# Differential attention heads: fp32 products against three f16 products of halves and remainders

## What is computed

```python
def block(args):
    q_blk, i = args                      # 128 queries
    ...
    logits = jnp.einsum('bqhmd,bkhmd->bhmqk', q_blk, k).astype(jnp.float32) * scale + bias
    p = jax.nn.softmax(logits, axis=-1)
    attn = p[:, :, 0] - lam * p[:, :, 1]
    return jnp.einsum('bhqk,bkhd->bqhd', attn.astype(v.dtype), v)
```

## Time and profile before

| what | before |
| --- | --- |
| median of 3 runs | 2670.33 us (2670.31 to 2670.44) |
| span of the profiled execution | 2668.5 us |
| PE busy | 2656.6 us, 100% |
| DVE busy | 1822.5 us, 68% |
| ACT busy | 1337.7 us, 50% |
| POOL busy | 136.5 us, 5% |

### The profile page before, as it was taken

One profiled execution on the slowest core, in us unless ns is written; L12 is line 12 of the kernel. 1 busy time (PEld: TensorE's weight loads), 2 busy tenths in 40 slices (PEclk: granted clock), 3 DMA queues, 4 the chain that ended last, 5 costly groups with the idle time before them and its releaser, 6 DMA issues.

```text
span 2668.5 us, 45121 instructions
## 1 busy us (share of the span) xinstructions
PE 2656.6 (100%) x17772; PEld 1741.6 (65%) x17772; DVE 1822.5 (68%) x2792; ACT 1337.7 (50%) x2284; POOL 136.5 (5%) x119
## 2 busy tenths in 40 slices
PE   9999999999999999999999999999999999999999
PEld 6886476654688646886476654688646556465664
DVE  7995385666899528994385665899526786557854
ACT  5664265552566425663265542566424654336452
POOL 1000012100100001000022100100000002000020
PEclk9999999999999999999999999999999999999999
DMA  5443321223344333443322223444323232321312
GB/s 170 115 121 107 122 80 59 88 67 104 91 120 116 116 98 95 121 115 107 122 80 67 81 74 104 116 125 111 121 100 119 72 95 72 111 84 64 111 64 87
DMA packets 313358, 266.23 MB, mean 100 GB/s; under 512 B 8796, under 2 KB 276316, under 8 KB 312576
## 3 DMA queue, kind: packets, MB, share of 16 engines
q1 hardware_dynamic: 310192, 254.31, 30.8%
q10 hardware_dynamic: 2416, 7.84, 1.1%
q0 software_dynamic: 608, 2.11, 0.3%
HBM read 257.40 MB, written 4.21 MB: 98 GB/s over the span
## 4 chain that ended last, share of the span: by engine, by line
PE 97%; DVE 1%; DMA 0%; DVEq 0%; ACT 0%; SPq 0%; issue 0%; ACTq 0%
PE pu L473 15%; PE pu L475 15%; PE pu L474 15%; PE pm L473 6%; PE pm L475 6%; PE pm L474 6%; PE pu L596 6%; PE pu L598 6%; PE pu L597 6%; PE pm L596 2%; PE pm L598 2%; PE pm L597 2%; PE pm L912 2%; PE pm L668 2%; PE pm L898 1%; PE pm L926 1%
## 5 line engine op out<-in xcount | busy, mean ns | idle before, releaser
L1105 DVE SCALAR_TENSOR_TENSOR w_lo<-stage,w_hi 128x2048 f16<-128x2048 f32 (+1 forms) x152 | 342.9, 2256 | 367.0 <-ACT w_hi L1885 363.3
L1885 ACT ACTIVATE w_hi<-stage 128x2048 f16<-128x2048 f32 (+1 forms) x143 | 265.9, 1859 | 529.4 <-PE pm L475 377.9
L473 PE MATMUL pu<-h_hi,w_hi 128*128 128x512 f16 x912 | 346.3, 380 | 0.0
L475 PE MATMUL pu<-h_hi,w_lo 128*128 128x512 f16 x912 | 345.6, 379 | 0.0
L474 PE MATMUL pu<-h_lo,w_hi 128*128 128x512 f16 x912 | 345.6, 379 | 0.0
L473 PE MATMUL pu<-w_hi,arena 128*128 128x512 f16 x512 | 194.0, 379 | 0.0
L474 PE MATMUL pu<-w_lo,arena 128*128 128x512 f16 x512 | 194.0, 379 | 0.0
L475 PE MATMUL pu<-w_hi,arena 128*128 128x512 f16 x512 | 194.0, 379 | 0.0
L473 PE MATMUL pm<-w_hi,arena 128*128 128x512 f16 x512 | 194.0, 379 | 0.0
L474 PE MATMUL pm<-w_lo,arena 128*128 128x512 f16 x512 | 194.0, 379 | 0.0
L475 PE MATMUL pm<-w_hi,arena 128*128 128x512 f16 x512 | 194.0, 379 | 0.0
(11 more groups left out here) (345 smaller groups left out, 6222.4 us busy)
## 6 DMA issues: line engine op xcount, KB each, us to landing
stage<-in_w_in_dram SPq DMA_DIRECT2D x144, 512.0 KB, 4.5
stage<-in_w_ffn_gate_dram SPq DMA_DIRECT2D x88, 512.0 KB, 3.9
stage<-in_w_ffn_up_dram SPq DMA_DIRECT2D x88, 512.0 KB, 5.1
stage<-in_w_ffn_down_dram SPq DMA_DIRECT2D x80, 512.0 KB, 4.0
stage<-in_w_out_dram SPq DMA_DIRECT2D x40, 512.0 KB, 4.2
stage<-in_w_ffn_down_dram SPq DMA_DIRECT2D x16, 256.0 KB, 4.2
stage<-in_w_branch_hgrn_dram SPq DMA_DIRECT2D x8, 512.0 KB, 3.4
stage<-in_w_branch_attn_dram SPq DMA_DIRECT2D x8, 512.0 KB, 4.6
```

The source lines that it names most:

```text
L473: nc.tensor.matmul(ps, w1, r_hi, start=first, stop=False)
L475: return nc.tensor.matmul(ps, w2, r_hi, start=False, stop=last)
L1105: V.scalar_tensor_tensor(out=w_lo[:, s, 0:n], in0=stage[:, s, 0:n], scalar=WSCALE, in1=w_hi[:, s, 0:n], op0=ALU.mult, op1=ALU.subtract).th ...
L1885: A.activation(w_hi[:, s, 0:n], stage[:, s, 0:n], ACT.Copy, scale=WSCALE).then_inc(hi_split, 1)
```

## The change

In the second block, for the differential heads alone:

- The evacuation of aq, ak and av units yields two f16 tiles, the rounded part and the remainder, scaled by 64. ScalarE writes the rounded part (new semaphore `part_hi`), in `mixer2` ahead of its `hi` for that unit; VectorE then writes the remainder in place of its evacuation.
- `scores2` makes each map's product in three f16 matmuls; those of the two maps alternate.
- `taken` writes the rounded part of the transposed probabilities and signals `pt_hi`; the new `probs_low(q - 1)` on VectorE, behind `probs2(q)`, writes their remainder and signals `pt_ready`.
- `head_out2` is three f16 matmuls for each of the 16 fp32 ones. Retention keeps the old form under the name `head_out_wide`.
- The scale 1/4096 of the products is taken back in the addition of the bias (now a three-operand instruction) and in ScalarE's copy of the head's output.

```diff
--- before.py
+++ after.py
@@ -92,6 +92,10 @@
 U_FFN, U_MIX = FFN_SLOTS - 1, MIX_ALL - 1
 
 
+SPLIT2 = ("aq", "ak", "av")
+SS = 1.0 / (ASCALE * ASCALE)
+
+
 ACT_KINDS = ("hf", "hq", "hg", "gate", "ag", "bg", "cg")
 
 
@@ -113,6 +117,7 @@
 PER2 = dict(split=24, land0=32 * 12, land1=32 * 12, hi_split=24, unit_done=23, evac=MIX2_DVE, evac_a=MIX2_ACT, pre_act=2, act_done=2, y_park=4, y_done=4,
             dec_pre=4, dec_done=4, sc_done=16, mx_ready=16, ex_done=16, p_ready=16, pt_done=16,
             pt_ready=16, o_rc=8, o_done=8, o_sq=8, o_rt=8, o_rb=8, o_cp=8, m_ready=12, rot_ready=2, rot_land=64, dup_land=32, ret_done=16, ret_ready=16, pw_land=16,
+            part_hi=6, pt_hi=16, 
             pool_sum=1, pool_in=4, pool_done=4, pool_free=1, x_ready=4, rx=4, xn_ready=4, tp_done=8, hh_ready=8, h_ready=8)
 
 
@@ -254,6 +259,9 @@
         toep = f32(72.25, A_HEADS, TW)
         dec, dec2 = f32(86.25, TW), f32(89.75, TW)
         AT = f32(93.25, NB, T)
+        (daq_hi, daq_lo), (dak_hi, dak_lo) = ((v[:, 0::2], v[:, 1::2]) for v in (f16(0, 8, T), f16(8, 8, T)))
+        AT_hi, AT_lo = f16(93.25, NB, T), f16(97.25, NB, T)
+        dV_hi, dV_lo = f16(16, NB, T), f16(20, NB, T)
 
         rel_hot, rel_row = f32(0, 2 * T)[0:32], f32(85, 2 * T)[0:A_HEADS]
         rel_tab = f32(8, A_HEADS)[0:32]
...
@@ -360,6 +370,16 @@
         end_bias = sem("end_bias")
         end_inv = sem("end_inv")
         end_half = sem("end_half")
+
+        def halves2(kind, part, banks):
+
+            dst = {"aq": (daq_hi, daq_lo), "ak": (dak_hi, dak_lo), "av": (dV_hi, dV_lo)}
+            out_hi, out_lo = dst[kind]
+            scale = DS * ASCALE * (0.125 if kind == "aq" else 1.0)
+            if kind in ("av", "bv"):
+                cols = slice(part * 256, part * 256 + 256)
+                return [(out_hi[:, b:b + 2, cols], out_lo[:, b:b + 2, cols], banks[b // 2][:].rearrange("p (b c) -> p b c", b=2), scale) for b in (0, 2)]
+            return [(out_hi[:, 2 * part + e], out_lo[:, 2 * part + e], banks[e][:], scale) for e in range(2)]
 
         x_in = a["x"].rearrange("(b p) d -> p b d", p=P)
 
@@ -887,15 +907,25 @@
             def scores2(i):
 
                 hd, b = divmod(i, NB)
-                for m in (1, 0) if i in (8, 12) else (0, 1):
+                parts = (daq_hi, dak_hi), (daq_hi, dak_lo), (daq_lo, dak_hi)
+
+                def part(m, j):
+
+                    r = slice(64 * m, 64 * m + 64)
+                    return nc.tensor.matmul(pm[2 * (i % 2) + m][:], parts[j][0][r, hd, b * P:(b + 1) * P], parts[j][1][r, hd], start=j == 0, stop=j == 2)
+
+                order = (1, 0) if i in (8, 12) else (0, 1)
+                for m in order:
                     if m == 0 and i >= 2:
                         pe.wait_ge(pt_ready, t.at("pt_ready", i - 1))
                     if m == 1 and i % 4 == 2 and i > 2:
                         pe.wait_ge(o_sq, t.at("o_sq", i // 4))
                     if m == 1 and i in (8, 12):
                         pe.wait_ge(o_cp, t.next("o_cp"))
-                    r = slice(64 * m, 64 * m + 64)
-                    last = nc.tensor.matmul(pm[2 * (i % 2) + m][:], daq[r, hd, b * P:(b + 1) * P], dak[r, hd], start=True, stop=True)
+                    last = part(m, 0)
+                for j in (1, 2):
+                    for m in order:
+                        last = part(m, j)
                 last.then_inc(sc_done, 1)
 
             def transpose2(i):
@@ -906,11 +936,21 @@
                     last = nc.tensor.transpose(pm[2 * (i % 2)][:, c], src[:, c], ident[:])
                 last.then_inc(pt_done, 1)
 
-            def head_out2(ps, v_tok, hd):
+            def head_out_wide(ps, v_tok, hd):
                 for b in range(NB):
                     for kb in range(NB):
                         last = nc.tensor.matmul(ps[:, b * P:(b + 1) * P], AT[:, kb, b * P:(b + 1) * P], v_tok[:, kb, hd * P:(hd + 1) * P],
                                                 start=kb == 0, stop=kb == NB - 1)
+                last.then_inc(o_done, 1)
+
+            def head_out2(ps, v_hi, v_lo, hd):
+
+                pairs = (AT_hi, v_hi), (AT_hi, v_lo), (AT_lo, v_hi)
+                for b in range(NB):
+                    for kb in range(NB):
+                        for j, (l, r) in enumerate(pairs):
+                            last = nc.tensor.matmul(ps[:, b * P:(b + 1) * P], l[:, kb, b * P:(b + 1) * P], r[:, kb, hd * P:(hd + 1) * P],
+                                                    start=kb + j == 0, stop=kb == NB - 1 and j == 2)
                 last.then_inc(o_done, 1)
 
             def retention_scores(hd):
@@ -935,7 +975,7 @@
                         pe.wait_ge(p_ready, t.now("p_ready") + 1)
                     else:
                         pe.wait_ge(o_cp, t.next("o_cp"))
-                    head_out2(pm[1], dV, (q - 5) // 4)
+                    head_out2(pm[1], dV_hi, dV_lo, (q - 5) // 4)
                 if 1 <= q <= 16:
                     transpose2(q - 1)
                 if q in (7, 11, 15):
@@ -961,7 +1001,7 @@
                         pe.wait_ge(evac, t.at("evac", 2 + evacuated(MIX2_ORDER.index(("bv", hd // 2)) + 1, False, MIX2_ORDER)))
                     if hd:
                         head_turn(pm[1], tc[:, (hd - 1) % 2])
-                    head_out2(pm[0], bV, hd)
+                    head_out_wide(pm[0], bV, hd)
                 if q == POOL_SLOT:
                     pe.wait_ge(pw_land, t.next("pw_land", 16))
                     pe.wait_ge(pool_in, t.next("pool_in", 4))
@@ -1654,7 +1694,7 @@
                 v.wait_ge(sc_done, t.next("sc_done"))
                 first = 3 * P - b * P
                 for m in range(2):
-                    V.tensor_tensor(Lm[:, m], pm[2 * (i % 2) + m][:], toep[:, hd, first:first + T], ALU.add)
+                    V.scalar_tensor_tensor(out=Lm[:, m], in0=pm[2 * (i % 2) + m][:], scalar=SS, in1=toep[:, hd, first:first + T], op0=ALU.mult, op1=ALU.add)
                 v.drain()
                 V.reduce_max(small[:, 0:2], Lm[:], AX.X)
                 v.drain()
@@ -1671,6 +1711,13 @@
                 v.drain()
                 V.scalar_tensor_tensor(out=Lm[:, 0], in0=Lm[:, 1], scalar=small[:, 7:8], in1=Lm[:, 0],
                                        op0=ALU.mult, op1=ALU.add).then_inc(p_ready, 1)
+
+            def probs_low(i):
+
+                v.wait_ge(pt_hi, t.next("pt_hi"))
+                c = slice(i % NB * P, (i % NB + 1) * P)
+                V.scalar_tensor_tensor(out=AT_lo[:, :, c], in0=pm[2 * (i % 2)][:].rearrange("p (k c) -> p k c", k=NB), scalar=ASCALE, in1=AT_hi[:, :, c],
+                                       op0=ALU.mult, op1=ALU.subtract).then_inc(pt_ready, 1)
 
             def split_out2(k):
                 v.drain()
@@ -1701,6 +1748,8 @@
                 between()
                 if q < 16:
                     probs2(q)
+                if 1 <= q <= 16:
+                    probs_low(q - 1)
                 if q == 17:
                     decay_exponents(0)
                 if 0 <= hd < B_HEADS and step == 0:
@@ -1746,7 +1795,12 @@
                     pending.append(evacuated(n + 1, True, MIX2_ORDER))
                 else:
                     v.wait_ge(unit_done, t.next("unit_done"))
-                if kind in ("av", "bv"):
+                if kind in SPLIT2:
+                    v.wait_ge(part_hi, t.next("part_hi"))
+                    for out_hi, out_lo, bank, scale in halves2(kind, part, banks):
+                        last = V.scalar_tensor_tensor(out=out_lo, in0=bank, scalar=scale, in1=out_hi, op0=ALU.mult, op1=ALU.subtract)
+                    last.then_inc(evac, 1)
+                elif kind in ("av", "bv"):
                     dst, first = dV if kind == "av" else bV, part * 256
                     for b in range(NB):
                         last = normed(dst[:, b, first:first + 256], banks[b // 2][:, (b % 2) * 256:(b % 2) * 256 + 256])
@@ -2217,7 +2271,7 @@
 
                 s_.wait_ge(pt_done, t.next("pt_done"))
                 b = i % NB
-                A.activation(AT[:, :, b * P:(b + 1) * P], pm[2 * (i % 2)][:].rearrange("p (k c) -> p k c", k=NB), ACT.Copy).then_inc(pt_ready, 1)
+                A.activation(AT_hi[:, :, b * P:(b + 1) * P], pm[2 * (i % 2)][:].rearrange("p (k c) -> p k c", k=NB), ACT.Copy, scale=ASCALE).then_inc(pt_hi, 1)
 
             def mixer2_slot(q):
                 ret, step = divmod(q - RET_SLOT, 2)
@@ -2237,7 +2291,7 @@
                     if k >= 2:
                         s_.wait_ge(m_ready, t.at("m_ready", k - 1))
                     s_.wait_ge(o_done, t.next("o_done"))
-                    A.activation(tc[:, k % 2], ps[:], ACT.Copy).then_inc(o_sq, 1)
+                    A.activation(tc[:, k % 2], ps[:], ACT.Copy, scale=SS if k < A_HEADS else 1.0).then_inc(o_sq, 1)
                 if 1 <= q <= 16 and q not in (8, 12):
                     taken(q - 1)
                 if ends:
@@ -2255,6 +2309,12 @@
             def mixer2(l):
                 hi_after_tail()
```

(8 more changed lines are left out.)

## The result

The changed kernel takes 2711.85 us (median of 4 runs, 2708.82 to 2712.53) against 2670.32 (4 runs); the ratio is 1.0153 (1.0139 to 1.0168). The forecast was 2709, the range 2698 to 2726. So the loss of 41.5 us was foretold within 3 us. But some of its terms were wrong: TensorE saves less than forecast, a waiting slot is shorter than forecast, and one rival, the clock, came true beside the forecast.

A forecast was written before the change was run, and what follows sets the result against it. TensorE, busy the whole span, was taken as the bound; new waits for VectorE outweigh its savings, plus 19.3 us a layer, 38.5 in two, on the 2668.5 us span: 2707, plus 1.8 to the median, 2709 us; range 2698 to 2726.

The forecast's parts named there:

- the clock: Rival: TensorE's clock falls at its new waits before scores; 2713 to 2726 us, middle 2717; 15%.
- What TensorE saves: f16 products save 0.42 us per score pair and 0.91 per head output, 20.7 us over two layers, were that all.
- 81 ns for each such matmul: Rival: 128-column matmuls in head outputs take 81 ns, not 56; 1.2 us more in 8 outputs, 2719 us; 4%.
- The ring: Scores of slot q+1 wait for VectorE's slot q, then the remainder of q-1: 8.37 us with a low half between.
- Late rounding: Slots 0, 2, 6: VectorE's evacuation waits for ScalarE's rounding behind exponentials; 10.9 us in 2 and 6, 17.3 from scores 0 to 2.
- The head slots: Slots 5, 9 and 13, with a head's output on TensorE: 9.02 us, above VectorE's time, TensorE saving 1.33.
- Faster, since the remainder is ready before TensorE returns: Rival: the wait before the scores hides below 6.36 us a slot, leaving only the 20.7 us saving: 2650 us; 6%.
- Products that don't overlap: Rival: f16 score pairs don't run beside each other, costing 1.30 us instead of 0.65; 2726 us; 11%.

The follow-up runs named there:

- early rounding and scores only: Changed kernel with only the scores in f16 parts and ScalarE rounding aq and ak units ahead of the exponentials: 2660.78 us, ratio 0.9964.
- head outputs alone: Changed kernel with scores back in fp32 and plain aq and ak evacuation; only head outputs in f16 parts: 2703.41 us, ratio 1.0126.
- kept busy: Changed kernel with superfluous f16 matmuls in TensorE's waits ahead of the scores of slots 2, 3, 7 and 13: 2706.98 us.
- early rounding: Changed kernel with ScalarE rounding aq, ak or av units ahead of the exponentials of the slot that evacuates them: 2691.91 us, ratio 1.0079.
- the experiment on their order: Changed kernel with one map's three f16 score products issued in succession, then the other's, instead of alternating: 2712.42 us.
- two runs with GpSimd's remainder: Changed kernel, rounding ahead of exponentials, probabilities' remainder on GpSimd: 2664.69 us; on top, bank emptied ahead of exponentials in slots 6, 8, 10, 12, 14: 2677.28 us.
- remainder first: Changed kernel with VectorE's remainder of slot q-1 ahead of the probability steps of slot q: 2688.53 us, ratio 1.0070.

## Why the prediction was right

**What TensorE saves.** Head outputs: 2.68 us (the start of L952 at 2108.15 to the transposes at 2110.83), forecast 2.66 to 2.68. The Trainium skill, "TensorE: Matmul & The Clock Gate", Back-to-back issue gap, has 81 ns for each such matmul, on which one rival rested; the trace disagrees: 2.68 us over 48 is 56 ns, as in the earlier trace rows.

```profile
2108.15 2.84 PE L952 MATMUL pm<-arena 128*128 128x128 f16 x48
2110.83 0.61 PE L936 MATMUL pm<-ident,ta 128*128 128x128 f32 x4
```

Scores: mis-sized. I put three steps of 0.216 us for a pair and left out the change over to the next full-height matmul. The third pair starts 0.44 us after the first's 2066.25; the projection matmul behind it starts 0.31 later, not 0.22:

```profile
2066.70 0.38 PE L915 MATMUL pm<-arena 64*128 64x512 f16 x2
2067.01 0.39 PE L493 MATMUL pu<-h_hi,w_hi 128*128 128x512 f16 x1
```

This 0.1 us is in every slot, and with it a pair saves 0.30 us and not 0.42: over 32 slots 3.8 us of gain that wasn't there. It shows alone where nothing waits, in the run with early rounding and scores only. The fp32 pair's 1.06 had it too, which is why I should have compared like with like: successive records of L926 start 0.43 apart, so 0.86 of the 1.06 are steps, and 0.2 lie around them. The Trainium skill, "TensorEngine Tiling (Array Packing)", Key Properties, says that a change of tiling mode drains TensorE; the trace agrees in kind, with these 0.1 us.

**The ring.** The step "the scores of slot q+1 wait for the remainder behind L1672 of slot q" held in full: the changed kernel's list of waits names it, moving the remainder gave 23.3 us back, and head outputs alone, with the ring, lose 33.1. Its length was put too long, by 0.2 us. With the clock up, a slot with a low half is 8.15 us ("kept busy", slot 3) and not 8.37: the additions cost nothing more as three-operand instructions (6.56 us to the end of L1712, no 0.13), the remainder's last 0.60 not 0.67, and TensorE follows in 0.06 instead of 0.15; against that, scores to additions 0.94 instead of 0.86. My bound for the additions came from L1672, whose operands all lie in SBUF; L1697 reads PSUM, as L1657 did, and takes 0.69 us as that did.

**Late rounding.** Forecast 10.9 us in slots 2 and 6, measured 10.6 with the clock up; 17.3 for slots 0 and 1, measured 16.8. Held: early rounding gave 19.9 us, some 4 of them the clock's.

**The head slots.** Forecast 9.02, measured 9.2 with the clock up; TensorE-bound as said, and longer by the 0.1 of the scores' change over in the main.

**The clock.** Here a rival of mine came true beside the forecast. I gave it 15% and a price of 4 to 17 us. It falls in each layer at the same four places, around the scores of slots 2 and 3, between slots 6 and 7 and in slot 13, and costs 5 us by the medians and 8 by the profiled executions. Scores at half clock hold TensorE 1.40 us, 0.64 more, as the rival had it. By the sum: with the clock up a layer is 131.1 us, 2.5 under the forecast of 133.6; the clock adds 3.9, and 135.0 is 1.4 over it. The sum without a clock term was about 5 us too high for two layers, and the clock's 5 to 8 took its place: so the forecast of the mechanism was right, and the closeness of the number is in part luck. Why a wait of 2.2 us brings a fall in one place and not in another is open: in the changed kernel the one ahead of the scores of slot 13 does; with early rounding the same wait there doesn't, and the one of 2.2 us ahead of slot 9 does. The prediction also reads the clock of the kernel before as low once; it is low a second time, after TensorE's last work (0.72 over 2663 to 2668.5 us), where it costs nothing. The Trainium skill, "TensorE: Matmul & The Clock Gate", What's actually happening, says that TensorE's clock drops after it idles and is restored by sustained activity; the trace agrees, with 0.50 behind the waits of 4.0 and 2.6 us and 1.00 again some microseconds on.

**The other rivals.** Faster, since the remainder is ready before TensorE returns: no. Products that don't overlap: no, and the experiment on their order shows that it doesn't even matter.

## What to carry to other kernels

When a step is split in two and the second half moves to another engine, look at what its semaphore releases and at what stands ahead of it in that engine's order: 0.68 us of work put behind a slot's last step made slots 3, 4, 10 and 14 0.8 to 1.4 us longer with the clock up, and slots 2 and 6, with late rounding, 3.8; ahead of the slot's last four steps the same work made slots 3, 4, 10 and 14 0 to 0.7 longer. Where TensorE is busy 100% of the time and another engine's steps through a slot are nearly as long (6.56 of 6.78 us here), first take the half of such a change that adds least to the other engines: the scores alone, with the rounding put where ScalarE stood idle, made the kernel 0.36% faster. All of it together made it 1.5% slower as first written, and 0.2% faster with the remainder on GpSimd. A wait on TensorE of some microseconds can have a second price, the clock behind it: 5 to 8 us in all here.

## What the runs showed of the hardware that I had not expected

- Two sets of three 64-row f16 products, each set in its own half of the rows, take 0.76 us whether they are issued alternating or one set after the other. The Trainium skill, "TensorEngine Tiling (Array Packing)", Key Properties, says that different tiles can load weights and multiply in parallel; the trace agrees, and this is more than I had drawn from the fp32 rows.
- A three-operand VectorE instruction with one operand in PSUM takes 0.69 us for 512 columns, the same as the addition it replaces; with all operands in SBUF it takes 0.75.
- A VectorE step with two large operands in SBUF and GpSimd's subtraction of two tiles in SBUF don't share: the one that starts second is held up. In the two runs with GpSimd's remainder, each of the 21 such VectorE steps that start during a subtraction ends 0.55 us behind it (L1716 at 2110.68: 1.62 us instead of 0.75; L1716 at 2160.82: 1.27; L1734: 1.65 instead of 0.75). A subtraction that starts during a VectorE step ends 1.0 us behind it (1.65 us instead of 1.16 at 2116.28), and that step keeps its 0.75. The additions, with one operand in PSUM, keep 0.69 beside a subtraction. The Trainium skill, "GPSIMD Engine Reference", Specifications, says that GpSimd shares its SBUF interfaces with VectorE, and names two SBUF inputs as a case of contention; the trace agrees.
- The clock's falls repeat. In the changed kernel they are in both layers at the same slots, 344.8 us apart, where the layers are 344.6 apart; in "remainder first" the two layers differ. The stretches of the falls between slots 1 and 2 in the second layer (the first layer's stands above), and between slots 6 and 7 in both:

```profile
2419.90:2426.70 6.80, 5.11 (x15) 1.62 (x16) 4.23 (x7) 0.67 (x2) 0.00 (x0) 0.50 0.48 154
2122.90:2129.70 6.80, 5.10 (x15) 1.63 (x16) 4.93 (x8) 0.66 (x2) 0.00 (x0) 0.50 0.00 0
2467.80:2474.50 6.70, 5.27 (x16) 1.69 (x17) 4.90 (x7) 0.83 (x3) 0.00 (x0) 0.50 0.00 0
```
